# Reading the moving columns as interleaved runs in six stages of a four-layer float32 kernel

## What is computed

```python
h = rmsnorm(x, g_pre[i])
u, z = split(h @ w_in[i])                    # 2048 -> 4096 and 4096
y = pool_mixer(u, pool_w, ...)               # layer 0: windowed mean minus token, then four 1024x1024 maps
y = rglru(causal_depthwise_conv(u, ...))     # layer 1: conv, then 16 heads of two 256x256 gate maps
y = y * silu(z)
o = y @ w_out[i]                             # 4096 -> 2048
x = x + rmsnorm(o, g_post[i])
gate = sigmoid(rmsnorm(x, g_ple_in[i]) @ w_ple_gate[i])
x = x + rmsnorm((p[i] @ w_ple[i]) * gate, g_ple_out[i])
```

## Time and profile before

| what | before |
|---|---|
| time, median of 3 runs | 3235.34 us (3235.27 to 3237.26) |
| the profiled execution's own time, its span from first to last instruction | 3231.5 us |
| what lies around the span (median less span) | 3.8 us |
| PE busy | 3224.2 us |
| PEld busy | 3067.1 us |
| DVE, ACT, POOL busy | 2245.0, 1673.9, 745.3 us |
| mean granted TensorE clock | 1.000 of full speed |

### The profile page before, as it was taken

How to read it: one execution, slowest core, us unless ns; L and a number is a source line. 1 busy time by engine, 2 the same in 40 slices (tenths; PEclk the granted TensorE clock), 3 DMA queues, 4 the chain that set the end, 5 groups by cost and what they waited for, 6 DMA issues and landing times.

```text
span 3231.5 us, 57755 instructions
## 1 busy us (share of the span) xinstructions
PE 3224.2 (100%) x24078; PEld 3067.1 (95%) x24078; DVE 2245.0 (69%) x2890; ACT 1673.9 (52%) x2082; POOL 745.3 (23%) x784
## 2 busy tenths in 40 slices
PE   9999999999999999999999999999999999999999
PEld 9999999999999999999899988889999999888889
DVE  7986654588888844887978655555568887555554
ACT  5344444565588844655655444444456554444443
POOL 2632320054544400332423200000114332000000
PEclk9999999999999999999999999999999999999999
DMA  7565665556666565555555566665665554666665
GB/s 248 183 203 191 195 225 195 178 190 216 196 194 192 196 224 194 188 191 195 169 182 170 170 196 199 193 201 193 194 201 174 177 176 157 195 196 198 194 198 174
DMA packets 171316, 621.66 MB, mean 192 GB/s; under 512 B 19376, under 2 KB 21424, under 8 KB 170672
## 3 DMA queue, kind: packets, MB, share of 16 engines
q1 hardware_dynamic: 165888, 601.96, 57.4%
q10 hardware_dynamic: 4880, 14.97, 1.2%
q0 software_dynamic: 288, 1.05, 0.1%
HBM read 611.61 MB, written 5.24 MB: 191 GB/s over the span
## 4 chain that ended last, share of the span: by engine, by line
PE 99%; DVE 1%; DMA 0%; ACT 0%; issue 0%; ACTq 0%; DVEq 0%
PE banks L648 20%; PE banks L600 13%; PE banks L589 13%; PE banks L590 13%; PE banks L665 10%; PE pm L600 5%; PE pm L589 5%; PE pm L590 5%; PE banks L752 2%; PE banks L730 2%; PE banks L732 2%; PE pm L752 2%; PE pm L732 2%; PE pm L730 2%; PE pm L800 0%; PE pm L926 0%
## 5 line engine op out<-in xcount | busy, mean ns | idle before, releaser
L1522 DVE TENSOR_TENSOR w_lo<-raw,w_hi 128x1024 fp32r<-128x1024 f32 x1144 | 1469.9, 1290 | 857.9 <-ACT w_hi L1056 851.5
L1056 ACT ACTIVATE w_hi<-raw 128x1024 fp32r<-128x1024 f32 x1143 | 1204.3, 1058 | 1089.7 <-PE banks L665 460.9
L589 PE MATMUL banks<-xs,w_hi 128*128 128x256 f32 x2468 | 579.4, 277 | 0.0
L590 PE MATMUL banks<-xs,w_hi 128*128 128x256 f32 x2468 | 578.1, 277 | 0.0
L648 PE MATMUL banks<-w_hi,xs 128*128 128x512 f32 x2048 | 493.5, 381 | 0.0
L590 PEld LDWEIGHTS banks<-xs,w_hi 128*128 128x128 f32 x2468 | 463.8, 188 | 0.3
L589 PEld LDWEIGHTS banks<-xs,w_hi 128*128 128x128 f32 x2468 | 463.8, 188 | 0.3
L648 PEld LDWEIGHTS banks<-w_hi,xs 128*128 128x128 f32 x2048 | 383.8, 188 | 68.2
L600 PE MATMUL banks<-xs,w_lo 128*128 128x256 f32 x2468 | 338.8, 279 | 0.0
L600 PEld LDWEIGHTS banks<-xs,w_lo 128*128 128x128 f32 x2468 | 305.7, 188 | 3.6 <-issue 2.5
L665 PE MATMUL banks<-w_lo,xs 128*128 128x512 f32 x1024 | 270.6, 384 | 0.0
(11 more groups left out here) (405 smaller groups left out, 5418.1 us busy)
## 6 DMA issues: line engine op xcount, KB each, us to landing
raw<-weights SPq DMA_DIRECT2D x1143, 512.0 KB, 3.6
wide<-x_in ACTq DMA_DIRECT2D x1, 2048.0 KB, 8.8
x_scratch<-wide ACTq DMA_DIRECT2D x1, 2048.0 KB, 12.5
wide<-x_scratch ACTq DMA_DIRECT2D x1, 2048.0 KB, 9.3
wide<-x_in ACTq DMA_DIRECT2D x3, 512.0 KB, 6.6
out_x<-wide SPq DMA_DIRECT2D x3, 512.0 KB, 5.4
g_v<-x_scratch ACTq DMA_DIRECT2D x2, 512.0 KB, 4.9
w_st<-w_s ACTq DMA_DIRECT2D x2, 512.0 KB, 4.6
```

The costliest lines, as they stand in the source:

```text
L589: nc.tensor.matmul(bank, w_hi[:, slot, w], x[:, 0:T], start=(k + t == 0), stop=False)
L590: nc.tensor.matmul(bank, w_hi[:, slot, w], x[:, T:2 * T], start=False, stop=False)
L1056: nc.scalar.activation(w_hi[:, slot, :], raw[:, slot, :], ACT.Copy).then_inc(hi_done, 1)
L1522: nc.vector.tensor_tensor(w_lo[:, slot, :], raw[:, slot, :], w_hi[:, slot, :].bitcast(F32), ALU.subtract).then_inc(lo_done, 1)
```

## The change

Two new functions describe the same 256 floats in another order. With form (c, f), `in_runs` takes runs of f floats, one out of every c, in c passes: (4, 4) takes 4 floats every 16 in four passes, (2, 8) 8 every 16 in two, (4, 8) 8 every 32 in four, (8, 4) 4 every 32 in eight.

```diff
+STORED = {"pooled": (4, 4), (0, "squared"): (2, 8), "lru": (4, 8), (1, "squared"): (8, 4)}
+SPREAD = {"silu": (4, 4), "conv": (8, 4)}
+def in_runs(a, form):
+    if form is None:
+        return a
+    return a.rearrange("p (g c f) -> p c g f", c=form[0], f=form[1])
+def in_order(a, form):
+    if form is None:
+        return a
+    return a.rearrange("p (c g f) -> p c g f", c=form[0], f=form[1])
...
             def products(s, i, ready, after, side):
...
-                    bank = product_bank(s, i, j)
+                    bank = in_runs(product_bank(s, i, j), SPREAD.get(s.name))
+                    form = SPREAD.get(s.name, p.form)
...
-                            nc.tensor.matmul(bank, w_hi[:, slot, w], x[:, 0:T], start=(k + t == 0), stop=False)
-                            nc.tensor.matmul(bank, w_hi[:, slot, w], x[:, T:2 * T], start=False, stop=False)
+                            nc.tensor.matmul(bank, w_hi[:, slot, w], in_runs(x[:, 0:T], form), start=(k + t == 0),
+                                             stop=False)
+                            nc.tensor.matmul(bank, w_hi[:, slot, w], in_runs(x[:, T:2 * T], form), start=False,
+                                             stop=False)
...
-                            ins = nc.tensor.matmul(bank, w_lo[:, slot, w], p.operand(i, k + t)[:, 0:T],
-                                                   start=False, stop=(k + t == p.depth - 1))
+                            ins = nc.tensor.matmul(bank, w_lo[:, slot, w],
+                                                   in_runs(p.operand(i, k + t)[:, 0:T], form), start=False, stop=(k + t == p.depth - 1))
...
+                form = s.products[0].form
...
-                link(nc.vector.tensor_copy(inner[:, m, 0:T], a))
-                nc.vector.tensor_tensor(inner[:, m, T:2 * T], a, inner[:, m, 0:T].bitcast(F32),
-                                        ALU.subtract).then_inc(tile_split, 1)
+                form = STORED["pooled"]
+                high, low, a = in_runs(inner[:, m, 0:T], form), in_runs(inner[:, m, T:2 * T], form), in_order(a, form)
+                link(nc.vector.tensor_copy(high, a))
+                nc.vector.tensor_tensor(low, a, high.bitcast(F32), ALU.subtract).then_inc(tile_split, 1)
...
-            def split(dest, source):
-                link(nc.gpsimd.tensor_copy(dest[:, 0:T], source))
-                nc.gpsimd.tensor_tensor(dest[:, T:2 * T], source, dest[:, 0:T].bitcast(F32),
-                                        ALU.subtract).then_inc(pool_done, 1)
+            def split(dest, source, form=None):
+                high, low, source = in_runs(dest[:, 0:T], form), in_runs(dest[:, T:2 * T], form), in_order(source, form)
+                link(nc.gpsimd.tensor_copy(high, source))
+                nc.gpsimd.tensor_tensor(low, source, high.bitcast(F32), ALU.subtract).then_inc(pool_done, 1)
```

More of the change, by code:

```diff
@@ L74, with __init__ @@
 class Product:
-    def __init__(self, depth, operand):
-        self.depth, self.operand = depth, operand
+    def __init__(self, depth, operand, form=None):
+        self.depth, self.operand, self.form = depth, operand, form
 class Stage:
@@ L344, in build @@
                 stage("window", [Product(ND, from_xs) for _ in range(4)], NI // 4, "p")
-                stage("pooled", [Product(8, lambda turn, k: inner[:, turn * 8 + k, :])
+                stage("pooled", [Product(8, lambda turn, k: inner[:, turn * 8 + k, :], STORED["pooled"])
                                  for _ in range(8)], NI // 8, "")
@@ L351, in build @@
                 for h in range(4):
-                    lru += [Product(2, lambda turn, k, h=h: inner[:, turn * 8 + 2 * h + k, :])
+                    lru += [Product(2, lambda turn, k, h=h: inner[:, turn * 8 + 2 * h + k, :], STORED["lru"])
                             for _ in range(4)] + [Product(ND, from_xs) for _ in range(2)]
@@ L355, in build @@
                       readers="AAAADD" * 4)
-            stage("squared", [Product(NI, from_inner) for _ in range(4)], ND // 4, "p", readers="AAAA")
+            stage("squared", [Product(NI, from_inner, STORED[layer, "squared"]) for _ in range(4)], ND // 4, "p", readers="AAAA")
             stage("plain", [Product(NP_, lambda turn, k: xs[:, ND - NP_ + k, :]) for _ in range(16)], 1, "",
@@ L729, in first_turn @@
                         bank, w = product_bank(s, j // 4, j % 4), slice(c * P, (c + 1) * P)
-                        nc.tensor.matmul(bank, w_hi[:, slot, w], operand[:, k, 0:T], start=(k == 0 and j < 4),
+                        nc.tensor.matmul(bank, w_hi[:, slot, w], in_runs(operand[:, k, 0:T], form),
+                                         start=(k == 0 and j < 4),
                                          stop=False, skip_group_check=True)
-                        nc.tensor.matmul(bank, w_hi[:, slot, w], operand[:, k, T:2 * T], start=False, stop=False,
+                        nc.tensor.matmul(bank, w_hi[:, slot, w], in_runs(operand[:, k, T:2 * T], form), start=False, stop=False,
                                          skip_group_check=True)
@@ L751, in first_turn @@
                         bank, w = product_bank(s, j // 4, j % 4), slice(c * P, (c + 1) * P)
-                        ins = nc.tensor.matmul(bank, w_lo[:, slot, w], operand[:, k, 0:T], start=False,
+                        ins = nc.tensor.matmul(bank, w_lo[:, slot, w], in_runs(operand[:, k, 0:T], form), start=False,
                                                stop=(k == s.products[0].depth - 1), skip_group_check=True)
@@ L2359, in post @@
                         split(inner[:, m, :] if s.name == "silu" else y_abc[:, m + first_tile, :],
-                              act[:, j % 4, :])
+                              act[:, j % 4, :], STORED[0, "squared"] if s.name == "silu" else None)
                     elif s.name == "latent":
@@ L2368, in post @@
                         gp.wait_ge(res_ready, m + (s.base["q"] + 1))
-                        split(inner[:, m, :], wide[:, m, :])
+                        split(inner[:, m, :], wide[:, m, :], STORED["lru"])
                     elif s.name == "squared":
@@ L2410, in split_z @@
                         gp.wait_ge(res_ready, z + (named[1, "lru"].base["q"] + 1))
-                        split(inner[:, z, :], act[:, j, :])
+                        split(inner[:, z, :], act[:, j, :], STORED[1, "squared"])
                 def gelu_inner(m):
```

## The result

The changed kernel takes 3289.24 us (median of 4 runs, 3287.17 to 3291.43) against 3235.31 us before: +53.9 us, a ratio of 1.0166 with a 95% interval of 1.0152 to 1.0181. It is slower, 31 us above the upper end of the range.

The account below looks back on a forecast made before the run. PE's matmul rhythm was taken to bound the kernel. Four terms, 0 + 0 + 0 + 0, left the forecast at the median before, 3235.3 us, with a range of 3211 to 3258 us.

Parts of the forecast that it names:

- What bounds the kernel: Whole kernel: PE busy 3224.2 of 3231.5 us at full clock; its matmul rhythm, 113.3 ns each, sets the end.
- the count of 6912 matmuls: Six stages: 4224 stored plus 2688 spread matmuls of 256 columns, 783 us at 113.3 ns.
- Term 1: PE reading moving columns in runs, all six stages: 0, bounded by a 23 us gain and a 32 us loss.
- A: Forecast case: rhythm stays at 113.3 ns in all six stages, 3235.3 us, own range 3231 to 3240; chance 0.40.
- The row by token: Stages by token, 512 columns read as 4 floats out of 16: 220.0 ns, 6.7 over the columns, taken as nearest operation.
- the upper bound of 4.6 ns per matmul: Loss bound for reading in runs, from zb of layer 2 at 117.9 ns; 32 us on all 6912 matmuls.
- The prediction's own sign of being wrong: Forecast is wrong if the stored stages alone move by more than 1 ns per matmul.
- Term 2: PE writing the bank in runs, silu and conv: 0, upper bound 274 us.
- D: Much slower: the bank takes runs at half rate in silu and conv, 3509 us; chance 0.05.
- Terms 3 and 4: DVE splitting in runs in window, 0 (bound +15 us); POOL splitting in runs in silu, conv, lru, 0.
- B: Faster: runs remove part of the 6.7 ns and the loads' 110 ns becomes the bound, 3212.3 us; chance 0.34.
- C: Slower: runs throw PE into its second rhythm, 117.9 ns; 3267 us with all six stages, 3247.7 with spread ones; chance 0.17.

Follow-up runs that it names:

- experiment 5: Changed kernel, but in squared of layer 0 PE reads tiles stored by (8, 4) in a row and writes the bank in runs; stretch 174.3 us.
- second survey: Changed kernel with other forms: pooled (4, 16), silu (2, 32), squared (16, 8) and (8, 16), conv (2, 64), gates (2, 4); squared of layer 0 123.4 ns per matmul.
- experiment 10: Changed kernel with other forms, computing only 64 or 32 of 128 output features per tile in five stages; (8, 4) beside 64: 121.9 ns mean.

## Why the prediction was wrong

**What bounds the kernel**: right. PE's rhythm is the whole of it, before and after, and the count of 6912 matmuls carries the sum: 53.6 us of 53.9 are in the six stages.

**Term 1** is the step that failed. It said "The simplest reading is a cost of the pair of weight load and matmul, and not of the columns' order", and priced all forms at 0. The runs show the order's price instead: 1.1 ns for (4, 4), 6.7 for (2, 8), 6.0 for (4, 8), 13.3 for (8, 4). The step fails by taking one equal excess, 6.7 ns in both rows, for a cost that no order changes. Two errors lie in it. First, a row with another number of columns and another order was taken as a control, when two things differed at once. Read in a row, 512 columns would have shown 228.6 ns and not 220.0, and that the order matters; the text named this under A as an accident that could be, and it was one. Second, one form stood for the change's four. The row by token is (4, 4), the cheapest of the interleaved ones that the change uses, and the upper bound of 4.6 ns per matmul came from an unchanged instruction in its other rhythm. It bounded nothing of a new pattern, and so the range ended at 3258. The prediction's own sign of being wrong was the right one: the stored stages moved by more than 1 ns per matmul, squared by 6.6 and 13.3.

**Term 2**: right, 0. The bank's runs are free (experiment 5), spread and stored forms cost the same, and D is gone. The rule of the Trainium skill named there ("PSUM — Partial Sum Buffer", Specifications), that any pattern that isn't contiguous slows matmuls significantly, does not hold here for runs of 4 floats: 174.3 us for 1536 matmuls with and without.

**Terms 3 and 4**: right, 0. DVE's split keeps 536 and 711 ns, POOL's copy and subtraction 1329 and 767 ns against 1298 and 772.

**The rivals.** B is refuted: none of the fourteen forms goes under 113.3 ns. C had the sign and a part of the mechanism. It priced a fall into the second rhythm of 117.9 ns at 32 us for all stages; that fall did happen, but in the z products of lru, which read in a row, and is worth 3.4 us. The other 50 us are the forms' own steady prices, which no rival had.

**What stays open** is why a form costs what it costs. The runs show that the price depends on the form, with the load unchanged, and on the load's length and step, with the form unchanged; whether the two reads collide or a part of the load is not covered, they don't show. They show no rule from which 113.3, 119.0 and 113.3 ns beside loads of 128, 64 and 32 columns would follow, or the order of the forms, or which of two steady values a stage takes.

## What to carry to other kernels

Read the moving operand of a 256-column fp32r matmul in a row; the one form tried with runs of fewer than 4 floats took almost twice the time; for 512 columns runs of (4, 4) are worth their trouble, 220.0 ns against 228.6. Price a new access pattern by that very pattern: a row with other columns or another step did not carry over here. A trial with a different form in each stage, between stages left alone, prices many at once. Look at the start-to-start distance along the stage and not at its mean alone, since some stages held two values. After any such edit look at the stages behind it as well: runs in za cost 3.8 us in unchanged code behind it.

## What was not expected of the hardware

- The matmul's price has steady values that depend on the order in which 256 floats are read: from 113.3 to 135.2 ns in runs of four floats or more, and 220.0 ns in runs of two.
- A weight load counts even where PEld has time to spare: read with a step of 2 floats it lengthens a 512-column matmul by 2.7 to 6.7 ns. A load of 64 columns instead of 128 made matmuls in a row slower, 119.0 ns.
- The second rhythm of lru's z products ended where two extra matmuls of 128 columns stand: 2.83 us a unit up to them, 2.72 us from then on. In the second survey the matmuls of conv, by (2, 64), go from 113.3 to 117.8 ns after a short stop of PE at 820 us, and back to 113.3 at such a pair at 868 us. But a pair can also be followed by a slower value: 116.7 and then 124.4 ns in experiment 10. That the pair is the cause was not tried by itself.
